# Attention scores of eight units as three one-pass products of high and low parts, held in the rings of the weights

## Chip, cores and metric

One core of a Trainium2 chip runs the whole program in one launch. The metric is the device time in microseconds, the median of the runs. The engines, as the profile names them: PE (matrix products; PEld are its weight loads), DVE (vector), ACT (scalar), POOL (GpSimd), SP (issues the weight transfers). Each engine works through its own list in order and waits on semaphores. PSUM is the memory that PE writes to, in 8 banks of 512 float32 columns.

## The reference

Two model blocks, one behind the other, on 256 latent tokens and (in the first block) 256 context tokens of width 2048, all float32. The first block has two layers with three kinds of attention heads side by side; latent queries read latent and context keys (512), context queries read context keys alone (256). In the second layer the context queries are left out, since nothing reads them.

```python
u = h @ w_in
qa, ka, va, qb, kb, vb, cq, ckv, kpe, z = jnp.split(u, split_points(), axis=-1)
...
# A: 8 heads of 64, neighbourhood window and a bias table; B: 12 heads of 64 over 4 key heads, band, sink
# C: 6 heads of 128 + 64 channels
s_loc = jnp.einsum('bqkgd,bjkd->bkgqj', qi, ki, preferred_element_type=jnp.float32) * scale
s_ctx = jnp.einsum('bqkgd,bckd->bkgqc', qi, kc, preferred_element_type=jnp.float32) * scale
p = jax.nn.softmax(s, axis=-1)
o = p @ v
...
x = x + gate[:, None] * merge_out(o_a, o_b, o_c, z, w_out[l])     # (y * silu(z)) @ w_out
```

The second block (pooling, a short convolution, gates, a feed-forward part of 5632) is not touched by the change.

## The kernel before

*Large products.* Every weight matrix comes in chunks of 128 x 1024 float32 through four buffers (`raw`). A step `split` makes two parts of a chunk: ACT copies it into `whi` in the type float32r (line 1151, the high part), DVE subtracts that from the chunk into `wlo` (line 1566, the low part). Both are rings of three places, `whi[:, s]` and `wlo[:, s]` with s = m % RING for chunk m of the whole program. The activations have high and low parts as well, and a product is the sum of three one-pass products (high x high, high x low, low x high; lines 908 to 910). A place of the ring is free when PE has used the chunk (`used`).

*The plan.* `make_plan` writes one list of steps, and each engine walks through the same list and does its share of each step. So the order in a step list is each engine's order. `pl.split()` puts the next chunk's split there.

*Attention.* A unit is a pair of heads of a kind. There are 13, in the order

```python
UNITS = (("B", 0), ("B", 1), ("C", 0), ("B", 2), ("B", 3), ("C", 1), ("B", 4), ("B", 5), ("A", 0), ("C", 2), ("A", 1),
         ("A", 2), ("A", 3))
```

numbered 0 to 12 here. A unit is worked in slots of 128 queries: in layer 0 four (stream 0, the latent queries, with 512 keys, twice; stream 1, the context queries, with 256 keys, twice), in layer 1 two (512 keys). So layer 0 has 52 slots, layer 1 has 26. For each slot s the plan has the steps `score` and `att`:

- PE, `score(s)`: the two heads' scores, queries x keys, as plain float32 products of 64 rows each (line 1039; kind C at lines 1030 and 1033). It waits for the row maxima of slot s - 2.
- PE, `att(s)`: the values product of slots s - 5 and s - 4 if slot s - 4 ends a stream (lines 1055, 1062), then the transposes of the probabilities of slot s - 2, head 0 and head 1 (line 1081); they wait for the scaled probabilities and for the copies of slot s - 3.
- DVE, `score(s)`: adds the mask and takes the row maximum (line 1982), both heads. `att(s)`: reciprocal of the sums of slot s - 1 (1990), scaling of head 0 (1993), the copy of head 0's transposes of slot s - 2 out of PSUM (2000), and where a unit is finished the product of its output with the gate (2012).
- ACT, `score(s)`: exponentials and sums (1462), both heads. `att(s)`: the copy of head 1's transposes (1471).
- POOL: scales head 1 (2258), sinks and the bias tables of kind A (2208), and issues the transfers of gates (2173).

The queries and keys of kinds A and B lie in `T`, 128 rows by 512 tokens for a pair of heads (two heads of 64 channels).

*The end.* The last three slots also have a `make` step each: the high and low part of an output row for the output projection `wout` (ACT line 1451, DVE line 1969). Then `att` steps alternate with the first chunks of `wout`. The first two splits of `wout` stand behind the two slots of unit 2, stream 0; the third behind the first `att` step after the last slot. During attention nothing else uses the rings.

Of the kernel before, what the change touches and what calls it, by code (L numbers as in the profile page):

```python
# [4 lines left out]
F32 = mybir.dt.float32  # L5
F32R = mybir.dt.float32r
ALU = mybir.AluOpType
ACT = mybir.ActivationFunctionType
# [5 lines left out]
L = 256  # L14
DEPTH = 2
# [23 lines left out]
RING = 3  # L39
# [16 lines left out]
def rows_of(kind, tile):  # L56

    return {"A": [tile], "B": [4 + tile], "C": [10 + 2 * tile, 11 + 2 * tile]}[kind]


Y_ORDER = [y for unit in UNITS for y in rows_of(*unit)]


# [339 lines left out]
def make_plan():  # L403
# [49 lines left out]
    for l, (first, second, third) in enumerate(layers):  # L453
        if l:
            pl.add("scale", l, None)
            pl.seam("layer", l)
            pl.mod_queue(MOD_LAST)
            chunks = pl.chunks(first)
            next(chunks)
            next(chunks)  # L460
            pl.add("load_conditions", 2)
            for _ in chunks:
                g, c = pl.last_chunk
                if g is first[1] and c == 4:
                    pl.add("conditions", 2)
                if g.id > first[1].id and (c % 2 or g.kind in ("kvb", "ka")):
                    pl.mod()
            assert not pl.mods
        pl.add("rq", l)
        pl.latents(second)  # L470
        keys = second[-1]
        pl.left[l], pl.keys[l], pl.queries[l] = pl.owner, keys, second[2]
        pl.turn, pl.owner = 1 - keys.base // 4, {0: None, 4: None}
        slots = slots_of(l)
        pl.add("load_gates", l)
        for s in range(len(slots)):
            pl.add("score", l, slots, s)
            pl.add("att", l, slots, s)
            if s == 0:
                pl.add("key_make", keys, (2, 3))  # L480
            if s == 1:
                pl.add("key_turn", keys, 2)
                pl.add("key_turn", keys, 3)
            if slots[s].unit == 2 and slots[s].stream == 0:
                pl.split()
            if s >= len(slots) - 3:
                pl.add("make", third[0], s - len(slots) + 3)
        chunks = pl.chunks(third, 3)
        for s in range(len(slots), len(slots) + 4):
            pl.add("att", l, slots, s)  # L490
            next(chunks)
        if l == 0:
            pl.mod_queue(MOD_SEAM)
            pl.add("load_conditions", 1)
        pl.add("attended", l, slots)
        for _ in chunks:
            g, c = pl.last_chunk
            if l == 0:
                if g.index == 0 and c == 6:
                    pl.add("conditions", 1)  # L500
                if g.index and (g.index < 3 or c < g.ending):
                    pl.mod(2 if g.index < 3 and c == 0 else 1)
        assert not pl.mods
        pl.flush()
# [11 lines left out]
def build(nc, d):  # L516
# [131 lines left out]

    def key_nope(head):
        return HF[:, head, :]  # L650

    def query_rope(tile):
        return HF[:, 12 + tile, :]
# [153 lines left out]
    def tensor_engine(PE):  # L807
# [210 lines left out]
        def score(l, slots, s):  # L1018
# [8 lines left out]
            if t.kind == "C":  # L1027
# [4 lines left out]
                for h in range(2):  # L1032
                    PE.matmul(out[h], query_rope(t.tile)[half[h], qs], key_rope(t.tile)[half[h], ks], start=False,
                              stop=True, tile_position=(64 * h, 0), skip_group_check=True).then_inc(
                        *scored.up((l, s, h)))
            else:
                q, k = (T_QA + t.tile, T_KA + t.tile) if t.kind == "A" else (T_QB + t.tile, T_KB + t.tile // 3)
                for h in range(2):
                    PE.matmul(out[h], T[half[h], q, qs], T[half[h], k, ks], start=True, stop=True,  # L1039
                              tile_position=(64 * h, 0)).then_inc(*scored.up((l, s, h)))  # L1040
# [101 lines left out]
    def scalar_engine(AC):  # L1142
        def split(m):
            g, c, n = pl.splits[m]
            s = m % RING
            width = min(g.kpc, g.kt - c * g.kpc) * g.width
            AC.wait_ge(*raw_in[pl.homes[n]].at(n))
            if m >= RING:
                was = pl.splits[m - RING]
                AC.wait_ge(*used.at(was[0].id, was[1]))  # L1150
            AC.activation(whi[:, s, 0:width], raw_of(n)[:, 0:width], ACT.Copy).then_inc(*hi.up((g.id, c)))  # L1151

        def ada_row(g):
# [299 lines left out]
        def score(l, slots, s):  # L1453
            t = slots[s]
            st_ = stat[:, s % 4, :, :]
            for h in range(2):
# [4 lines left out]
                    AC.wait_ge(*p_ev.at("sink", l, s))  # L1461
                AC.activation(p_, p_, ACT.Exp, bias=st_[:, 0, h:h + 1], scale=-1.0, accum_out=st_[:, 1, h:h + 1]).then_inc(*exped.up((l, s, h)))

        def att(l, slots, s):
            if 2 <= s < len(slots) + 2:
                t = slots[s - 2]
# [8 lines left out]
        for st in pl.steps:  # L1475
# [43 lines left out]
                att(*st[1:])  # L1519
            elif st[0] == "rq":  # L1520
                latent_roots(st[1])
            elif st[0] == "key_square":
                key_square(*st[1:])
            elif st[0] == "key_root":
# [27 lines left out]
    def vector_engine(VE):  # L1552
# [419 lines left out]
        def score(l, slots, s):  # L1972
            t = slots[s]
            for h in range(2):
# [3 lines left out]
                if t.kind == "A" and t.tile == 0 and t.stream == 0 and h == 0:  # L1978
# [3 lines left out]
                VE.tensor_tensor_reduce(p_of(t, h), PS[:, score_bank(l) + 2 * (s % 2) + h, 0:t.nk], mask_of(t, h), -1.0, first,  # L1982
                                        ALU.add, ALU.min, stat[:, s % 4, 0, h:h + 1]).then_inc(*maxed.up((l, s, h)))

        def att(l, slots, s):
            if 1 <= s <= len(slots):
                t = slots[s - 1]
# [27 lines left out]
        for st in pl.steps:  # L2015
# [43 lines left out]
                att(*st[1:])  # L2059
            elif st[0] == "rq":  # L2060
                VE.tensor_tensor(rq[:, :, 0], rq[:, :, 0], rq[:, :, 1], ALU.add).then_inc(*v_ev.up(("rq_sum", st[1])))
            elif st[0] == "key_square":
                key_square(*st[1:])
            elif st[0] == "key_root":
# [381 lines left out]
```

## Time and profile before

| what | value |
|---|---|
| median of 3 runs | 3156.88 us (3156.69 to 3157.13) |
| profiled execution, its time | 3160.49 us |
| its span | 3159.2 us |
| mean granted PE clock | 0.992 of full speed |
| PE / PEld / DVE / ACT / POOL busy | 98 / 87 / 60 / 42 / 9 % of the span |
| attention, layer 0 | about 692 to 850 us |
| attention, layer 1 | about 1478 to 1578 us |

The page's first part has the busy time of each engine, its second part the span in 40 slices, its fourth the chain of work that ended last, followed back from the end. Timelines list instructions by start in microseconds from the start of the span; "x4" are four records merged, with the time from the first start to the last end; in brackets stands how long the engine was idle before and what released it. A PE record's end is modelled and reaches past the next record's start, so the time that an instruction takes of PE's queue is read from start to start. A float32 product shows as two records. Windows give busy microseconds of each engine in a stretch.

### The profile page before, as it was taken

To read this page: it belongs to the slowest core of one execution; us is meant where nothing else is said; L and a number is where in the kernel's file an instruction comes from. 1 tells how busy PE (TensorE), PEld (TensorE's weight loads), DVE (VectorE), ACT (ScalarE), POOL (GpSimd) and SP (SyncE) were. 2 spreads that over 40 slices of the span, in tenths; PEclk is the share of its full clock that TensorE was granted. 3 is DMA by queue.
4 is the path that set the end of the run, shared out by engine and by line. 5 is a ranking of instruction groups with operands and counts; after the bars stand their busy time and mean duration, and the time that the engine had idled before them with its cause. 6 is when DMAs were issued, how large, how long until landed. Compare 5 with 4: busy or idle time off the path is not lost.

```text
span 3159.2 us, 51244 instructions
## 1 busy us (share of the span) xinstructions
PE 3093.2 (98%) x21274; PEld 2759.7 (87%) x21274; DVE 1893.5 (60%) x2949; ACT 1340.6 (42%) x2075; POOL 295.6 (9%) x386
## 2 busy tenths in 40 slices
PE   7999999999999999998999999999999999999998
PEld 3788888875688898886599999999999999999998
DVE  4376676377768566446757755555556555555445
ACT  4422333355532643345544444344444444444443
POOL 0001000017421010002710000000000000000000
PEclk9999999999999999999999999999999999999999
DMA  9776554221166387432064555555554555555554
GB/s 398 290 236 217 180 192 161 79 74 67 41 253 220 121 300 245 154 112 103 31 204 167 180 184 186 185 190 194 191 193 166 199 194 194 193 195 194 194 194 160
DMA packets 154984, 571.27 MB, mean 181 GB/s; under 512 B 17760, under 2 KB 17888, under 8 KB 152192
## 3 DMA queue, kind: packets, MB, share of 16 engines
q1 hardware_dynamic: 147312, 533.71, 49.2%
q0 software_dynamic: 7440, 34.28, 3.0%
q8 instruction: 168, 2.75, 0.3%
q14 instruction: 64, 0.52, 0.0%
HBM read 555.34 MB, written 12.58 MB: 180 GB/s over the span
## 4 chain that ended last, share of the span: by engine, by line
PE 92%; DVE 2%; DMA 2%; ACT 2%; issue 1%; POOL 1%; SPq 0%; DVEq 0%; ACTq 0%
PE ps L908 20%; PE ps L910 20%; PE ps L909 20%; PE ps L897 7%; PE ps L899 7%; PE ps L898 7%; DMA sb_raw<-in_stream 2%; PE ps L1081 2%; PE ps L1039 1%; PE ps L1062 1%; PE ps L817 1%; PE ps L1055 1%; POOL sb_p L2258 1%; PE ps L1030 1%; DVE sb_p L1982 1%
## 5 line engine op out<-in xcount | busy, mean ns | idle before, releaser
L1566 DVE TENSOR_TENSOR sb_wlo<-sb_raw,sb_whi 128x1024 fp32r<-128x1024 f32 (+1 forms) x809 | 983.5, 1217 | 974.9 <-ACT sb_whi L1151 973.3
L1151 ACT ACTIVATE sb_whi<-sb_raw 128x1024 fp32r<-128x1024 f32 (+1 forms) x813 | 853.9, 1051 | 1030.5 <-PE ps L910 781.0
L908 PE MATMUL ps<-sb_hn_hi,sb_whi 128*128 128x256 f32 (+4 forms) x2944 | 822.3, 279 | 4.4 <-DVE sb_hn_lo L1680 4.4
L909 PE MATMUL ps<-sb_hn_lo,sb_whi 128*128 128x256 f32 (+4 forms) x2944 | 820.9, 279 | 0.0
L910 PE MATMUL ps<-sb_hn_hi,sb_wlo 128*128 128x256 f32 (+4 forms) x2944 | 820.7, 279 | 0.0
L908 PEld LDWEIGHTS ps<-sb_hn_hi,sb_whi 128*128 128x128 f32 x2944 | 555.1, 189 | 5.2 <-DVE sb_hn_lo L1680 4.6
L910 PEld LDWEIGHTS ps<-sb_hn_hi,sb_wlo 128*128 128x128 f32 x2944 | 555.5, 189 | 0.0
L909 PEld LDWEIGHTS ps<-sb_hn_lo,sb_whi 128*128 128x128 f32 x2944 | 555.3, 189 | 0.0
L899 PE MATMUL ps<-sb_whi,sb_lo 128*128 128x512 f32 (+1 forms) x968 | 376.4, 389 | 0.0
L897 PE MATMUL ps<-sb_whi,sb_hi 128*128 128x512 f32 x896 | 356.0, 397 | 5.3 <-DVE sb_lo L1660 4.1
L898 PE MATMUL ps<-sb_wlo,sb_hi 128*128 128x512 f32 x896 | 350.0, 391 | 0.0
L908 PE MATMUL ps<-sb_hi,sb_whi 128*128 128x512 f32 (+1 forms) x992 | 333.1, 336 | 0.3 <-ACT sb_scr L1216 0.2
L909 PE MATMUL ps<-sb_lo,sb_whi 128*128 128x512 f32 (+1 forms) x992 | 330.6, 333 | 0.0
L910 PE MATMUL ps<-sb_hi,sb_wlo 128*128 128x512 f32 (+1 forms) x992 | 330.5, 333 | 0.0
L899 PEld LDWEIGHTS ps<-sb_whi,sb_lo 128*128 128x128 f32 x968 | 183.0, 189 | 37.1
L908 PEld LDWEIGHTS ps<-sb_hi,sb_whi 128*128 128x128 f32 x992 | 186.3, 188 | 26.7 <-issue 5.8
L897 PEld LDWEIGHTS ps<-sb_whi,sb_hi 128*128 128x128 f32 x896 | 169.1, 189 | 39.3 <-DVE sb_lo L1660 4.3
L910 PEld LDWEIGHTS ps<-sb_hi,sb_wlo 128*128 128x128 f32 x992 | 186.3, 188 | 19.5
L909 PEld LDWEIGHTS ps<-sb_lo,sb_whi 128*128 128x128 f32 x992 | 186.4, 188 | 19.0
L898 PEld LDWEIGHTS ps<-sb_wlo,sb_hi 128*128 128x128 f32 x896 | 169.2, 189 | 34.8
L908 PE MATMUL ps<-sb_ffn_hi,sb_whi 128*128 128x256 f32 x688 | 189.9, 276 | 0.0
L910 PE MATMUL ps<-sb_ffn_hi,sb_wlo 128*128 128x256 f32 x688 | 189.9, 276 | 0.0
(306 smaller groups left out, 4270.2 us busy)
## 6 DMA issues: line engine op xcount, KB each, us to landing
sb_raw<-in_stream SPq DMA_DIRECT2D x939, 512.0 KB, 3.4
sb_T<-in_stream SPq DMA_DIRECT2D x41, 512.0 KB, 10.7
sb_raw<-in_stream SPq DMA_DIRECT2D x25, 384.0 KB, 3.0
sb_T<-in_x SPq DMA_DIRECT2D x4, 1024.0 KB, 9.4
z_scratch<-sb_scr POOLq DMA_DIRECT2D x16, 256.0 KB, 3.8
sb_zb<-z_scratch POOLq DMA_DIRECT2D x16, 256.0 KB, 3.0
sb_bias<-in_bias POOLq DMA_DIRECT2D x4, 1024.0 KB, 6.0
x_scratch<-sb_T POOLq DMA_DIRECT2D x4, 1024.0 KB, 4.5
```

What stands on the lines that cost most here:

```text
L817: mm = PE.matmul(PS[t:t + 32, ada_bank(g), :], cond[:, k, :], raw_of(n)[:, 512 * j:512 * j + 512], start=k < 4, stop=k >= 12, tile_positio ...
L897: PE.matmul(o, xh[:, xt], wh, start=k == 0, stop=False)
L898: PE.matmul(o, xh[:, xt], wl, start=False, stop=False)
L899: mm = PE.matmul(o, xl[:, xt], wh, start=False, stop=k == g.kt - 1)
L908: PE.matmul(o, whi[:, s, w], xh, start=k == 0, stop=False)
L909: PE.matmul(o, whi[:, s, w], xl, start=False, stop=False)
L910: mm = PE.matmul(o, wlo[:, s, w], xh, start=False, stop=k == g.kt - 1)
L1030: PE.matmul(out[h], T[:, T_QN + head, qs], key_nope(head)[:, ks], start=True, stop=True, skip_group_check=True)
L1039: PE.matmul(out[h], T[half[h], q, qs], T[half[h], k, ks], start=True, stop=True, tile_position=(64 * h, 0)).then_inc(*scored.up((l, s, h)))
L1081: mm = PE.transpose(PS[:, turn_bank(l, h), kt * P:kt * P + P], p_of(t, h)[:, kt * P:kt * P + P], ident)
L1151: AC.activation(whi[:, s, 0:width], raw_of(n)[:, 0:width], ACT.Copy).then_inc(*hi.up((g.id, c)))
L1566: VE.tensor_tensor(wlo[:, s, 0:width], raw_of(n)[:, 0:width], whi[:, s, 0:width].bitcast(F32), ALU.subtract).then_inc(*lo.up((g.id, c)))
```

## The change

Eight units, all of kind A and those of kind B from tile 2 on (units 3, 4, 6, 7, 8, 10, 11, 12), get high and low parts of their queries and keys. These are put into a place of the rings `whi` and `wlo` (queries in columns 0 to 511, keys in 512 to 1023), and the scores become three one-pass products for each head. ACT makes the high parts in the first slot of the unit before (`operand_hi`), DVE the low parts in the second slot of that unit, stream 0 (`operand_lo`); both steps stand behind `score` and `att` of their slot. PE waits for `operand_lo` before the first score of a changed unit. The two splits of `wout` that stood in unit 2 move to unit 12, the last one, and their ring places wait for the scores of units 10, 11 (and the third one's for those of unit 12). Units 0, 1 and kind C stay as they are.

```diff
+PAIRED = [u for u, (kind, tile) in enumerate(UNITS) if kind == "A" or kind == "B" and tile > 1]
...
-            if slots[s].unit == 2 and slots[s].stream == 0:
+            ahead, first = slots[s].unit + 1, s == 0 or slots[s - 1].unit < slots[s].unit
+            if ahead in PAIRED and first:
+                pl.add("operand_hi", l, ahead)
+            if ahead in PAIRED and not first and slots[s - 1].qt == 0 and slots[s].stream == 0:
+                pl.add("operand_lo", l, ahead)
+            if slots[s].unit == PAIRED[-1] and slots[s].stream == 0:
                 pl.split()
...
+    def operands(l, u):
+        s = (third_first[l].m0 + PAIRED.index(u) + 1 - len(PAIRED) + 2) % RING
+        n, (kind, tile) = L if l else 2 * L, UNITS[u]
+        q, k = (T_QA + tile, T_KA + tile) if kind == "A" else (T_QB + tile, T_KB + tile // 3)
+        return ((T[:, q, 0:n], whi[:, s, 0:n], wlo[:, s, 0:n]),
+                (T[:, k, :], whi[:, s, 512:1024], wlo[:, s, 512:1024]))
+
+    def last_scored(l, u):
+        return scored.at(l, max(t.s for t in slots_of(l) if t.unit == u), 1)
...
+            elif t.unit in PAIRED:                                   # PE, score
+                if t.stream == 0 and t.qt == 0:
+                    PE.wait_ge(*v_ev.at("operand_lo", l, t.unit))
+                (_, qh, ql), (_, kh, kl) = operands(l, t.unit)
+                for i, (q, k) in enumerate(((qh, kh), (qh, kl), (ql, kh))):
+                    for h in range(2):
+                        mm = PE.matmul(out[h], q[half[h], qs], k[half[h], ks], start=i == 0, stop=i == 2,
+                                       tile_position=(64 * h, 0))
+                        if i == 2:
+                            mm.then_inc(*scored.up((l, s, h)))
...
+            if g.kind == "wout" and g.index == 0 and c < RING:       # ACT, split
+                AC.wait_ge(*last_scored(g.layer, PAIRED[c - RING]))
...
+        def operand_hi(l, u):                                        # ACT
+            j = PAIRED.index(u)
+            AC.wait_ge(*(last_scored(l, PAIRED[j - RING]) if j >= RING else used.at("done", pl.keys[l].id)))
+            for v, hi_, _ in operands(l, u):
+                ins = AC.activation(hi_, v, ACT.Copy)
+            ins.then_inc(*a_ev.up(("operand_hi", l, u)))
...
+        def operand_lo(l, u):                                        # DVE
+            VE.wait_ge(*a_ev.at("operand_hi", l, u))
+            for v, hi_, lo_ in operands(l, u):
+                ins = VE.tensor_tensor(lo_, v, hi_.bitcast(F32), ALU.subtract)
+            ins.then_inc(*v_ev.up(("operand_lo", l, u)))
```

## Rows read from the trace of the kernel before

**Rows 1.** The page: busy time, share of the span and instructions of each engine.

```profile
PE 3093.2 (98%) x21274; PEld 2759.7 (87%) x21274; DVE 1893.5 (60%) x2949; ACT 1340.6 (42%) x2075; POOL 295.6 (9%) x386
```

**Rows 2.** The page: chain of work that ended last, by engine.

```profile
PE 92%; DVE 2%; DMA 2%; ACT 2%; issue 1%; POOL 1%; SPq 0%; DVEq 0%; ACTq 0%
```

**Rows 3.** Windows: the attention stretches of both layers.

```profile
core 0: us, PE busy (x) PEld busy (x) DVE busy (x) ACT busy (x) POOL busy (x), PEclk, DMA share, GB/s
691.90:850.20 158.30, 148.51 (x860) 86.03 (x859) 124.23 (x394) 95.22 (x271) 99.05 (x110) 0.98 0.13 44
1478.00:1578.50 100.50, 92.06 (x503) 52.10 (x502) 77.67 (x205) 57.43 (x140) 68.89 (x72) 0.97 0.14 49
```

**Rows 4.** Timeline, layer 1, two units: start, us, engine, line, operation.

```profile
1555.23 1.09 PE L1081 MATMUL ps<-sb_const,sb_p 128*128 128x128 f32 x8
1555.92 0.69 DVE L2000 COPY sb_pt<-ps 128x512 f32<-128x512 f32 x1 [0.56 <-PE ps L1081]
1556.25 1.13 PE L1039 MATMUL ps<-sb_T 64*128 64x512 f32 x4
1556.53 0.42 DVE L2012 TENSOR_TENSOR sb_T<-ps,sb_zb 128x256 f32<-128x256 f32 x1
1557.31 1.09 PE L1081 MATMUL ps<-sb_const,sb_p 128*128 128x128 f32 x8
1559.39 1.95 PE L1062 MATMUL ps<-sb_pt,sb_va 128*64 128x256 f32 x16
1562.29 1.13 PE L1039 MATMUL ps<-sb_T 64*128 64x512 f32 x4
```

**Rows 5.** Timeline, PE, layer 0: scores of 256 keys, then transposes.

```profile
776.39 0.70 PE L1039 MATMUL ps<-sb_T 64*128 64x256 f32 x4
777.03 1.09 PE L1081 MATMUL ps<-sb_const,sb_p 128*128 128x128 f32 x8
```

**Rows 6.** Windows: one-pass products, of 512 and of 256 columns.

```profile
875.00:900.00 25.00, 25.00 (x112) 20.72 (x111) 8.37 (x9) 12.27 (x12) 4.35 (x5) 1.00 0.85 349
3000.00:3100.00 100.00, 100.00 (x885) 100.00 (x884) 49.77 (x51) 42.69 (x46) 5.17 (x7) 1.00 0.56 193
```

**Rows 7.** Timeline: weight loads of one slot's scores.

```profile
1556.25 0.30 PEld L1039 LDWEIGHTS ps<-sb_T 64*128 64x128 f32 x4 [0.17 <-issue]
```

**Rows 8.** Lines 1969 and 1451: ns min/median/max; then one of 256.

```profile
L1969 DVE TENSOR_TENSOR sb_lo<-sb_T,sb_hi x16: 680/684/693, 844.0 to 884.4; 128x512 fp32r<-128x512 f32 x16
L1451 ACT ACTIVATE sb_hi<-sb_T x16: 613/617/624, 843.3 to 883.0; 128x512 fp32r<-128x512 f32 x16
1571.00 0.42 DVE L1969 TENSOR_TENSOR sb_lo<-sb_T,sb_hi 128x256 fp32r<-128x256 f32 x1
```

**Rows 9.** Windows: one unit of kind A in layer 0.

```profile
827.91:837.74 9.83, 9.72 (x66) 5.29 (x65) 8.75 (x31) 6.84 (x20) 6.91 (x6) 1.00 0.18 56
```

**Rows 10.** Timeline, layer 1, unit 2: a split behind slot 5.

```profile
1500.76 1.04 ACT L1151 ACTIVATE sb_whi<-sb_raw 128x1024 fp32r<-128x1024 f32 x1
1500.94 1.23 PE L1081 MATMUL ps<-sb_const,sb_p 128*128 128x128 f32 x8
1501.84 1.22 DVE L1566 TENSOR_TENSOR sb_wlo<-sb_raw,sb_whi 128x1024 fp32r<-128x1024 f32 x1 [0.87 <-ACT sb_whi L1151]
1502.98 0.74 DVE L1982 CUSTOM_DVE_ANT_0 sb_p<-ps,sb_const,sb_nsink 128x512 f32<-128x512 f32 x1
```

**Rows 11.** Timeline: transposes ahead of the first output-projection chunk, both layers.

```profile
849.77 0.41 PE L1081 MATMUL ps<-sb_const,sb_p 128*128 128x128 f32 x2 [1.67 <-DVE sb_pt L2000]
1577.40 1.39 PE L1081 MATMUL ps<-sb_const,sb_p 128*128 128x128 f32 x8 [1.32 <-DVE sb_T L2000]
```

**Rows 12.** Timeline and windows: two gaps of PE and the clock.

```profile
697.47 0.41 PE L959 MATMUL ps<-sb_const,sb_lo_f 128*128 128x128 f32 x2 [3.60 <-DVE sb_lo_f L1869]
700.20:703.60 3.40, 3.15 (x14) 1.77 (x13) 2.85 (x10) 2.01 (x7) 2.60 (x3) 0.50 0.00 0
748.00:751.50 3.50, 1.82 (x12) 0.97 (x11) 3.26 (x6) 2.23 (x8) 3.50 (x6) 1.00 0.06 23
```

More of the change, by code:

```diff
@@ L650, in key_nope @@
         return HF[:, head, :]
+    def operands(l, u):
[6 more added lines that the diff above has]
+        return scored.at(l, max(t.s for t in slots_of(l) if t.unit == u), 1)
+    third_first = [next(g for g in pl.groups if g.kind == "wout" and g.layer == l) for l in range(DEPTH)]
     def query_rope(tile):
@@ L1035, in score @@
                         *scored.up((l, s, h)))
+            elif t.unit in PAIRED:
[8 more added lines that the diff above has]
+                            mm.then_inc(*scored.up((l, s, h)))
             else:
-                q, k = (T_QA + t.tile, T_KA + t.tile) if t.kind == "A" else (T_QB + t.tile, T_KB + t.tile // 3)
+                q, k = T_QB + t.tile, T_KB + t.tile // 3
                 for h in range(2):
@@ L1521, in scalar_engine @@
                 latent_roots(st[1])
+            elif st[0] == "operand_hi":
+                operand_hi(*st[1:])
             elif st[0] == "key_square":
@@ L2061, in vector_engine @@
                 VE.tensor_tensor(rq[:, :, 0], rq[:, :, 0], rq[:, :, 1], ALU.add).then_inc(*v_ev.up(("rq_sum", st[1])))
+            elif st[0] == "operand_lo":
+                operand_lo(*st[1:])
             elif st[0] == "key_square":
```

## The prediction, made before the changed kernel was built

> **What bounds the kernel now.** First the page's busy line and its chain of waits: the matrix engine (PE) works 98% of the span and is 92% of the chain [rows 1, 2]. A change pays only if it shortens PE's queue or keeps it from waiting. Then the two attention stretches: 158.3 us in layer 0 and 100.5 us in layer 1, PE busy 148.5 and 92.1 of them, the vector engine (DVE) 124.2 and 77.7 [rows 3]. So PE leads, but DVE is a close second at 78%. Last the timeline around one step from unit to unit in layer 1, because the change puts DVE work there [rows 4]: transposes of slot 17 at 1555.23, first score of the next unit at 1556.25, its transposes 1557.31, values 1559.39, the next unit's first score 1562.29. In these 6.04 us stand two scores of 1.06, two sets of transposes of 1.02 and, as the rest, values of 1.88. No PE row there carries a wait of weight; the 6.04 us of a unit are PE's own work.
>
> **Part 1, the scores.** One slot's scores are two float32 products of 64 rows, which the trace shows as four PE records that share the array in pairs. With 512 keys they take 1.06 us of PE's queue (1556.25 to 1557.31 [rows 4]), with 256 keys 0.64 us (776.39 to 777.03 [rows 5]). The difference is 0.42 us for 256 columns, which leaves about 0.21 us fixed. New are six one-pass products, three for each head. A one-pass product takes 25.0/112 = 0.223 us at 512 columns and 100/885 = 0.113 us at 256 [rows 6], so the float32 product streams its keys about four times, the new one three times. If the heads go on sharing the array, a slot takes 3/4 x 0.85 + 0.21 = 0.85 us and 3/4 x 0.43 + 0.21 = 0.53 us, so 0.21 and 0.11 us less. Changed are 8 units: 2 slots of 512 keys in each layer (32), 2 of 256 in layer 0 (16). Gross gain 32 x 0.21 + 16 x 0.11 = 8.5 us, 3.4 of it in layer 1. If the six ran in series it would be 6 x 0.223 + 0.21 = 1.55 and 6 x 0.113 + 0.21 = 0.89 us, a loss of 0.49 and 0.25 each, 19.7 in all: the other bound. I take the overlap, because the float32 records of the same tile positions show it.
>
> The weight loads are the doubtful point. The four loads of a slot's scores lie within 0.30 us of its start [rows 7], two for each half of the array, so a half takes a second load while its first product still streams. The Trainium skill, "TensorE: Matmul & The Clock Gate", section "Measured speedup vs the span model", says that a load overlaps running matmuls only when its row group differs. By that rule the second and third loads of a half would be exposed, and the gain would vanish; the 0.30 us speak against it here.
>
> **Part 2, the high and low parts.** For each unit the scalar engine (ACT) copies queries and keys, DVE subtracts. One piece of 512 columns costs DVE 0.68 us, of 256 0.42 us, ACT 0.62 us for 512 [rows 8]; started behind each other they take some 0.07 us less. Layer 0 (512 + 512): DVE 1.3 us. Layer 1 (256 + 512): 1.03 us. ACT's copies go into the first slot of the unit before and need about 1.0 to 1.2 us; after its last copy ACT waits for a score and a row maximum (0.85 + 0.1 + 0.6 us), so I cost them at 0 to 0.1.
>
> The place of the subtraction decides. It stands at the end of DVE's list for the second slot of the unit before, behind the copy of the transposes (L2000) and the gate product (L2012), and PE waits for it ahead of the next unit's first score.
>
> *Layer 1* has one stream, so that score is the very next thing PE does after those transposes. From their start at 1555.23: the copy can start at 1555.92, when the first half is through, the gate product at 1556.53 [rows 4], the subtractions at 1556.9, done at 1557.95, PE released at about 1558.05 instead of 1556.25. A stall of 1.8 us. Behind the stopped PE stand both scores, both sets of transposes and the values of the unit, and DVE has nothing to do until that score is there, so neither catches up. New period: 0.85 + 1.02 + 0.85 + 1.88 + 2.82 (to the release) = 7.42 us for 6.04, +1.4. Eight such steps: 8 x 1.8 = 14.6, and 0.66 more where the gated unit is of kind C (a second gate product [rows 4], 0.33 us behind the first, at two of the steps): 15.3 us. Less 16 x 0.21 = 3.4: **+11.9**.
>
> *Layer 0* has two streams, so two slots of 256 keys lie between subtraction and use; PE need not wait for it directly. But DVE is busy 8.75 us of a 9.83 us unit [rows 9]. With 1.3 more it has 10.05: DVE becomes the bound in the five units of kind A or B that carry a subtraction (3, 6, 7, 10, 11): +0.2 each at least, +0.3 taken for idle time that it can't fill, 1.5. Their score gain is gone in that figure. Units 4, 8 and 12 carry none and keep 2 x 0.21 + 2 x 0.11 = 0.64 each: -1.9. Units of kind C have long PE work and hide it. Layer 0: **-0.4** (all hidden would be -5.1; +0.5 a unit more, +0.6).
>
> **Part 3, the moved splits.** Two splits of output-projection chunks move from unit 2 to unit 12. Each is 1.05 us on ACT, then 1.22 us on DVE, which waits for ACT. In layer 1 at unit 2 the next row maximum starts at 1502.98, 2 us after its score ended at 1500.94 [rows 10]. Taking these away gives back 0.7 and 0.8 us. At unit 12 they hit the drain of the pipeline, where PE already waits 1.67 and 1.32 us for DVE's copies [rows 11]. Following the queue in layer 1: the subtraction puts the row maximum of slot 25 2.05 us later, so the copy of slot 23, so the transposes of slot 24; chunk 0 follows. **+2**. In layer 0 both splits stand before the row maxima of slots 49 and 50, each costs some 2 us and little is idle: **+4**. Their two loads are issued later too, but while DMA is little used (mean share 0.13 and 0.14 [rows 3]): 0. The bounds for both are nothing and 2 x 2.3 us a layer.
>
> **Sum** on the profiled span of 3159.2 us: layer 0 -0.4 + 4 - 0.7 = +2.9; layer 1 +11.9 + 2 - 0.8 = +13.1; together +16, a span of 3175. The profiled execution itself took 3160.49 us, 3.6 over the median of the runs, 3156.88; I put the difference on the median: **3173 us**, 0.5% slower.
>
> **Rivals.**
> *The clock falls (15%).* The moved splits stretch PE's waits at the ends of attention to about 3.0 and 3.4 us. A wait of 3.60 us at 697.47 was followed by a granted clock of 0.50 [rows 12], 1.2 GHz. A fall costs about half of 6.8 us: 3.4 us, two of them 6.8: 3176 to 3180. The 1.8 us stalls leave PE busy three quarters of the time; a stretch with 1.82 busy of 3.50 us kept clock 1.00 [rows 12], so I expect none there. The Trainium skill, "TensorE: Matmul & The Clock Gate", section "Why this matters for your kernels", advises against idle gaps over some 3 us between bursts of matmuls; the 3.60 us row agrees.
> *The six products don't overlap (7%).* Then the scores lose 19.7 us instead of gaining 8.5. Layer 1 pays it in full (16 x 0.70 = 11), layer 0 partly behind DVE (about 10): +37, near 3194. For it: no row has one-pass products on half the array. Against it: the pairs and the loads [rows 5, 7].
> *Half the stall (8%).* If DVE's queue is ahead of where I put it and the stall is near 0.9 us, layer 1 costs 5 us and the moved splits little: within 0.2%, 3158 to 3163.
> *Faster (4%).* The other side: the subtraction falls in time in which DVE is idle. Then only the 8.5 us count, 3148. It decides from the point where the subtractions end before the second half of the transposes, 0.5 us after the first. The copy ahead of them alone needs more [rows 4], so this wants another order of DVE's work than the code has.
> *The sum (66%)*, 3165 to 3182: half to one and a half times the split costs, the layer 1 stall at 1.6 to 2.2 us, and layer 0 from -3 to +3 beside it.
>
> The range 3164 to 3187 takes in the clock's case and leaves out 8% + 4% below and 7% above. 0.2% is 6.3 us, about what a measurement tells from no change: slower by more has 0.66 + 0.15 + 0.07 = 0.88, same 0.08, faster 0.04.
>
> **What the profile after would show.** Right: PE's first score of each changed unit in layer 1 waits some 1.8 us for DVE's subtraction, eight times, and the layer 1 stretch grows by 13 us to about 114; a changed slot of 512 keys takes about 0.85 us; in layer 0 those scores wait for nothing, units 6, 7, 10, 11 take about 10.1 us, with DVE nearly full; the waits before chunk 0 grow to 3 us or more. Wrong: slots of 1.2 us or more (no overlap), a granted clock of 0.50 inside layer 1's units, or waits under 1 us at the new scores. What could break it most: a DVE queue that runs in another order than I read.

## The result: 0.9% slower, in the place that was forecast, by more than was forecast

The changed kernel took 3184.27 us (median of 4 runs, 3179.5 to 3209.13), the kernel before beside it 3157.01 (3156.69 to 3158.66): ratio 1.0095, 95% interval 1.0056 to 1.0134. The forecast was 3173 us, a ratio of 1.005. Slower is right; 3184 lies inside the range of 3164 to 3187 and 11 us above its centre, and the ratio that the forecast stands for lies outside the interval.

The profiled execution of the changed kernel took 3179.5 us (span 3178.2). The page's busy line and its chain of waits, which answer to [rows 1] and [rows 2]:

```profile
PE 3092.3 (97%) x21370; PEld 2770.1 (87%) x21370; DVE 1909.5 (60%) x2981; ACT 1356.2 (43%) x2107; POOL 296.6 (9%) x386
...
PE 93%; DVE 3%; ACT 1%; issue 1%; DMA 1%; POOL 1%; SPq 0%; DVEq 0%; ACTq 0%
```

PE is busy as long as before in a span 19 us longer, so on the whole the added time is waiting. (Its busy time has slower products in it as well, as the filler experiment shows below.) The windows of the two attention stretches, from the first score to the first output-projection chunk, say where; under them four short windows of layer 1:

```profile
core 0: us, PE busy (x) PEld busy (x) DVE busy (x) ACT busy (x) POOL busy (x), PEclk, DMA share, GB/s
691.90:855.30 163.40, 148.12 (x923) 92.03 (x923) 133.37 (x411) 103.27 (x287) 99.67 (x110) 0.96 0.13 43
1478.30:1597.90 119.60, 96.16 (x544) 60.02 (x543) 82.95 (x221) 64.71 (x157) 69.59 (x72) 0.92 0.11 37
1510.00:1512.40 2.40, 1.42 (x8) 0.90 (x9) 1.13 (x3) 1.11 (x3) 2.40 (x4) 0.83 0.00 0
1512.40:1515.80 3.40, 3.40 (x16) 2.50 (x15) 2.68 (x8) 2.01 (x5) 2.55 (x4) 0.62 0.15 41
1530.50:1532.90 2.40, 0.79 (x4) 0.76 (x6) 1.46 (x2) 0.00 (x0) 1.65 (x4) 0.83 0.06 14
1532.90:1536.30 3.40, 3.40 (x19) 2.19 (x16) 2.50 (x7) 1.74 (x5) 0.93 (x1) 0.62 0.08 29
```

Layer 0's attention grew from 158.3 us [rows 3] to 163.4. Layer 1's took 102.2 us before (cut in the same way, from the first score at 1476.4; the window of [rows 3] begins 1.6 us after that score) and 119.6 after. Together that is +22.5 us where the forecast had +16. PE's granted clock over layer 1's stretch is 0.92 for 0.97, and the short windows show two of its falls, each at the end of a wait of PE.

The waits of PE in layer 1, by line; columns: engine and line, what was waited for, us in total, times, longest:

```profile
PE ps L1061 <- DVE sb_wlo L2028: 15.9, 8, 2.7
PE ps L978 <- DVE sb_lo_f L1909: 3.6, 1, 3.6
PE ps L1110 <- DVE sb_T L2046: 3.0, 1, 3.0
PE ps L1110 <- DVE sb_pt L2046: 0.7, 1, 0.7
```

L1061 is the new score, L2028 the subtraction `operand_lo`: eight waits, 15.9 us, as forecast (eight, 15.3). The wait of 3.0 us is the one for the last transposes, 1.32 before [rows 11]. The timeline shows first an undisturbed step, to be read against [rows 4], and then a disturbed one:

```profile
1567.83 1.09 PE L1110 MATMUL ps<-sb_const,sb_p 128*128 128x128 f32 x8
1568.52 0.69 DVE L2046 COPY sb_pt<-ps 128x512 f32<-128x512 f32 x1 [0.56 <-PE ps L1110]
1569.13 0.41 DVE L2058 TENSOR_TENSOR sb_T<-ps,sb_zb 128x256 f32<-128x256 f32 x1
1569.46 1.02 DVE L2028 TENSOR_TENSOR sb_wlo<-sb_T,sb_whi 128x256 fp32r<-128x256 f32 x2
1570.63 0.50 PE L1061 MATMUL ps<-sb_whi 64*128 64x512 f32 x2 [1.70 <-DVE sb_wlo L2028]
1571.52 1.09 PE L1110 MATMUL ps<-sb_const,sb_p 128*128 128x128 f32 x8
1578.11 0.51 PE L1061 MATMUL ps<-sb_whi 64*128 64x512 f32 x2 [1.70 <-DVE sb_wlo L2028]
...
1528.30 1.09 PE L1110 MATMUL ps<-sb_const,sb_p 128*128 128x128 f32 x8
1529.60 0.42 DVE L2058 TENSOR_TENSOR sb_T<-ps,sb_zb 128x256 f32<-128x256 f32 x1
1529.83 1.58 POOL L2256 TENSOR_TENSOR sb_bias<-sb_bias,sb_const 128x256 f32<-128x256 f32 x2
1529.93 2.03 DVE L2028 TENSOR_TENSOR sb_wlo<-sb_T,sb_whi 128x256 fp32r<-128x256 f32 x2
1532.11 0.80 PE L1061 MATMUL ps<-sb_whi 64*128 64x512 f32 x2 [2.72 <-DVE sb_wlo L2028]
1533.69 1.95 PE L1110 MATMUL ps<-sb_const,sb_p 128*128 128x128 f32 x8
```

In the first, DVE does its copy, its gate product and the subtraction behind each other after the transposes of 1567.83, and PE has nothing to do until 1570.63: a wait of 1.70 us and a unit of 7.48 us (1570.63 to 1578.11) for 6.04. Scores to transposes take 0.89 us (1570.63 to 1571.52) where the old ones took 1.06, so the products of the two heads do share the array (six in series would take 6 x 0.223 = 1.34 [rows 6]). In the second, the subtraction takes 2.03 us instead of 1.02 with POOL's L2256 running beside it. The wait is 2.72 us, and what follows runs at half the clock: 1.58 us for the slot's scores, 1.95 for eight transposes that take 1.09 above.

### The profile page after: what moved, and what is told of

Its sections match the earlier page's. It is cut to its first block, busy times and chain, and to the rows that moved or that the text cites. A ratio compares the mean times of both kernels' runs of the same rounds, so it can differ in the third digit from the quotient of the medians.

```text
span 3178.2 us, 51516 instructions
## 1 busy us (share of the span) xinstructions
PE 3092.3 (97%) x21370; PEld 2770.1 (87%) x21370; DVE 1909.5 (60%) x2981; ACT 1356.2 (43%) x2107; POOL 296.6 (9%) x386
## 4 chain that ended last, share of the span: by engine, by line
PE 93%; DVE 3%; ACT 1%; issue 1%; DMA 1%; POOL 1%; SPq 0%; DVEq 0%; ACTq 0%
PE ps L927 20%; PE ps L929 20%; PE ps L928 20%; PE ps L916 7%; PE ps L918 7%; PE ps L917 7%; PE ps L1110 2%; PE ps L1091 1%; PE ps L836 1%; PE ps L1061 1%; DMA sb_raw<-in_stream 1%; PE ps L1049 1%; PE ps L1084 1%; PE ps L1009 1%; DVE sb_wlo L1606 1%
```

## The experiments

The time of a whole run is a blunt measure here: runs of one kernel, the one before among them, differ by 30 us and more from one to the next, through a part that the change doesn't touch (last section). The lengths of the two attention stretches repeat within about a microsecond where the clock does. So each kernel is judged by them first. The table gives the time in us from the first score to the first output-projection chunk in one profile each, and in brackets how much of it passed at a granted clock of 0.50. The kernel before has a second profile to see how far the stretches repeat: they differ from the first by 0.8 and 0.9 us.

| kernel | layer 0 | layer 1 | sum | ratio of times (95%) |
|---|---|---|---|---|
| before | 158.3 (6.8) | 102.2 (6.8) | 260.5 | 1 |
| before, again | 159.1 (10.2) | 101.3 (0) | 260.4 | |
| changed | 163.4 (13.7) | 119.6 (18.0) | 283.0 | 1.0095 (1.0056 to 1.0134) |
| changed, second | 162.8 (17.6) | 116.4 (6.8) | 279.2 | 1.0096 (1.0052 to 1.0139) |
| changed, fourth | 164.1 (13.2) | 120.0 (17.6) | 284.1 | |
| changed, fifth | 163.4 (17.0) | 120.6 (23.9) | 284.0 | |
| subtraction early | 163.3 (10.8) | 100.4 (6.0) | 263.7 | 0.9988 (0.9955 to 1.0022) |
| splits moved alone | 161.3 (9.5) | 101.4 (3.6) | 262.7 | 1.0036 (0.9999 to 1.0072) |
| filler products | 164.2 (13.2) | 113.6 (5.4) | 277.8 | 1.0039 (1.0004 to 1.0074) |
| filler products, again | 163.4 (13.7) | 113.6 (5.1) | 277.0 | |
| plain scores, waits kept | 165.5 (11.3) | 117.8 (4.6) | 283.3 | 1.0109 (1.0048 to 1.0171) |
| layer 0 alone | 163.6 (9.8) | 103.0 (6.8) | 266.6 | 1.0015 (0.9991 to 1.0039) |
| layer 1 alone | 159.2 (10.2) | 119.9 (17.4) | 279.1 | 1.0063 (1.0030 to 1.0095) |
| layer 1 alone, again | 158.1 (6.8) | 119.5 (18.0) | 277.6 | |
| layer 1 alone, filler | 158.1 (6.8) | 113.2 (0) | 271.3 | 1.0028 (0.9987 to 1.0068) |
| six units, early | 159.0 (10.2) | 99.6 (3.4) | 258.6 | 1.0007 (0.9978 to 1.0035) |
| six units, layer 1 alone | 158.7 (6.8) | 99.5 (3.4) | 258.2 | 0.9998 (0.9958 to 1.0037) |

### The changed kernel again, and the subtraction moved forward

Two experiments on the main claim. The first is the changed kernel itself.

> The changed kernel as it is, once more, timed in more rounds. If the excess over the forecast 3173 us is a fixed cost, the runs lie close together near 3184 us. If part of it is the granted clock falling in the 1.7 us gaps, or a transfer that comes late in some runs, the runs spread by 5 to 30 us as the first four did (3179.5 to 3209.1 us), and their mean clocks differ.

The ratio came out the same, 1.0096, and the times spread as in the second case of the expectation, from 3182.75 to 3224.21 us (two more of the twelve ran at another clock throughout, see the last section). The profile has the same eight waits (16.6 us) but only one fall of the clock between units, and a layer 1 of 116.4 us.

The second does the same work at another place: copies two units ahead, subtraction at the start of the unit before.

```diff
             if ahead in PAIRED and first:
-                pl.add("operand_hi", l, ahead)
-            if ahead in PAIRED and not first and slots[s - 1].qt == 0 and slots[s].stream == 0:
                 pl.add("operand_lo", l, ahead)
+            if ahead + 1 in PAIRED and not first and slots[s - 1].qt == 0 and slots[s].stream == 0:
+                pl.add("operand_hi", l, ahead + 1)
```

> Only the place of the two steps is changed: the subtraction moves from the second slot of the unit before to its first slot, the copies one slot further ahead (second slot of the unit before that). The work is the same. Theory (the place makes the stall): PE's waits for the subtraction (15.9 us, 8 times in layer 1) go, and the falls of the clock inside layer 1 with them; scores keep their gain; about 3160 us, 3157 to 3164. Rival (the amount of work on the vector engine): no better than 3175 us. Rival (something outside attention became slower): layer 1's stretch gets shorter, the time stays above 3170 us.

Layer 1 fell to 100.4 us, below the kernel before, and the ratio to 0.9988; the median of 3167.20 us is above the 3157 to 3164 expected, but so is that of the kernel before beside it (3164.86). DVE does as much there as in the changed kernel (83.69 us of the stretch for 82.95), so it is the place of the subtraction, not its amount, that costs layer 1 its time. No score waits for DVE any more; the waits of PE in layer 1 and one unit of the timeline:

```profile
PE ps L1110 <- DVE sb_T L2046: 4.3, 3, 3.4
PE ps L978 <- DVE sb_lo_f L1909: 3.6, 1, 3.6
PE ps L1110 <- DVE sb_pt L2046: 1.3, 2, 0.7
...
1555.38 1.09 PE L1110 MATMUL ps<-sb_const,sb_p 128*128 128x128 f32 x8
1556.41 0.49 PE L1061 MATMUL ps<-sb_whi 64*128 64x512 f32 x2
1557.30 1.09 PE L1110 MATMUL ps<-sb_const,sb_p 128*128 128x128 f32 x8
1562.12 0.50 PE L1061 MATMUL ps<-sb_whi 64*128 64x512 f32 x2
```

The unit takes 5.71 us (1556.41 to 1562.12) for 6.04 before. Layer 0 stayed at 163.3, but not because the place does nothing there. Units 2 to 10 took 111.7 us (714.56 to 826.29) for 113.3 in the changed kernel and 111.9 with the moved splits alone. Unit 11 then took 12.29 us for 9.98, with a wait of 1.20 us for DVE's copy at 832.95 and a fall of the clock at 834.2.

### The moved splits alone

The kernel before, with the two splits at unit 12:

```diff
-            if slots[s].unit == 2 and slots[s].stream == 0:
+            if slots[s].unit == 12 and slots[s].stream == 0:
```

> The kernel before with the two splits of the output projection moved from unit 2 to unit 12 alone, no high and low parts of queries and keys. Theory: +6 us in the drains (4 in layer 0, 2 in layer 1), -1.5 us at unit 2, so about 3161 us. Rival: the moved splits cost nothing, 3157 us.

Layer 0 took 161.3 us (+3.0 on the first profile, +2.2 on the second), layer 1 101.4, no change. The median was 3175.53 us beside 3164.86, where +4.5 had been expected; its interval reaches from nothing to 0.7%. Behind the first score of unit 12, layer 0 took 16.96 us (836.21 to 853.17) for 12.46, which is +4.5 for the +4 expected in that drain. PE's wait for the last transposes of layer 1 grew from 1.32 us [rows 11] to 3.1, as the forecast had it. What was given back behind unit 2 paid for it: units 3 and 4 of layer 1 took 14.62 us for 16.44 in the second profile of the kernel before, 1.8 us less where 0.8 had been expected.

### Filler in the gaps: what the clock costs

PE runs two products that nobody reads in each of layer 1's eight waits. Their results are not used; everything else is as in the changed kernel.

```diff
                 if t.stream == 0 and t.qt == 0:
+                    if l:
+                        for _ in range(2):
+                            PE.matmul(PS[:, pl.keys[l].base + 3, :], ident, const[:, band0:band0 + 512], start=True, stop=True)
                     PE.wait_ge(*v_ev.at("operand_lo", l, t.unit))
```

> The changed kernel with PE kept busy in layer 1 while it waits for the subtraction: two float32 products of 512 columns (0.85 us each) on constants into an unused PSUM bank, ahead of each of the eight waits. They do no useful work. Theory (the excess over the forecast is the clock, which falls in the gaps): no granted clock of 0.50 between the units of layer 1, about 1.7 us less for each of the four falls of the changed kernel's profile, so 7 us less than the changed kernel and less spread between runs. Rival: the excess has another cause, then the time stays or grows by what the two products reach past the wait (0 to 3 us).

The trace shows these as plain float32 products, 1.88 us for the two, so they fill nearly the whole wait. The filler kernel's waits, a step of its timeline and its window of layer 1:

```profile
PE ps L1064 <- DVE sb_wlo L2031: 2.4, 5, 0.9
...
1548.79 1.04 PE L1113 MATMUL ps<-sb_const,sb_p 128*128 128x128 f32 x8
1549.67 1.88 PE L1059 MATMUL ps<-sb_const 128*128 128x512 f32 x4
1551.77 0.50 PE L1064 MATMUL ps<-sb_whi 64*128 64x512 f32 x2 [0.22 <-DVE sb_wlo L2031]
...
1482.30:1595.90 113.60, 103.74 (x575) 60.95 (x575) 83.33 (x221) 64.38 (x157) 69.12 (x72) 0.98 0.11 39
```

The first score comes 2.98 us after the start of the transposes (1548.79 to 1551.77); the same step without filler takes 3.07 (1549.05 to 1552.12). The wait is as long as ever, only filled. But no fall stands between two units any more, and layer 1 is 6.0 us shorter than in the first profile of the changed kernel, for the 7 expected. The two left are behind the wait for L1912 at the start, which the first profile of the kernel before has as well, and in the drain. Timed in the same set the ratios are 1.0039 and 1.0096, the same direction, with intervals that overlap.

Whether those falls are the usual case took more profiles.

> The change in layer 1 alone, and PE runs two one-pass products of 512 columns on a free bank while it would wait for the subtraction, ahead of each new unit's first score; nothing else differs from only_l1. Theory, the clock: in only_l1 layer 1's attention took 119.9 us with 17.1 us of it at a granted clock of about 0.5; with the gaps filled no fall stands between two units, at most that of the drain, and the stretch takes 113 to 115 us, as in the kernel with both layers and the filler (113.6); the timed median is 5 to 9 us under that of only_l1. Rival, the falls cost nothing of note, since the waits for DVE leave room for a slower PE: the stretch stays over 117 us, the time within 2 us of only_l1.

> The changed kernel with the filler products in layer 1's gaps, a second profile. Theory: no fall between units in any execution, 113 to 114.5 us for layer 1's attention, as in both profiles with a filler so far (113.6, 113.2). Rival, the filler's executions had luck: 116 us or more.

> The change in layer 1 alone, a second profile. Theory, falls are usual: 117 to 120 us for layer 1's attention with 10 us or more at the low clock. Rival: 114 to 116.5 us. Layer 0 158 to 159.5 us, as before the change.

> The changed kernel, a third profile. It says how often the clock falls between the units of layer 1 (17.2 us at the low clock in the first profile, 6.8 in the second). Theory, the falls are the usual case and cost about 3 us on top of the waits: layer 1's attention 116 to 120 us, with three or more falls between units. Rival, they were one execution's: 114 to 116.5 us and at most one fall. Layer 0 162 to 164 us in both.

> The changed kernel once more. Theory, the falls of the clock between the units of layer 1 are the usual case: layer 1's attention 117 to 120 us, 10 us or more of it at the low clock. Rival, they are rare: 114 to 116.5 us, at most 7 us at the low clock. Layer 0 162 to 164 us in both.

> The changed kernel once more, with the same two cases: 117 to 120 us for layer 1's attention with 10 us or more at the low clock, or 114 to 116.5 us with at most 7.

The third profile of the changed kernel can't be compared in length: that whole execution ran at a mean granted clock of 0.748 and took 3882.65 us. There too the clock fell further, to 0.50, behind five of the eight waits. The others settle it. Without filler five of six profiles have four or more falls of 3.4 us between units, and take 119.5 to 120.6 us; the sixth has one fall of 6.8 and takes 116.4. With filler, three of three have none and take 113.6, 113.6 and 113.2. The expectation of layer 1 alone with filler calls the filler products one-pass; they were not, as said. Timed, that kernel has a ratio of 1.0028 where layer 1 alone has 1.0063, again in the expected direction and with intervals that overlap. The windows of layer 1, changed kernel (fourth and fifth profile), layer 1 alone again, then layer 1 alone with filler:

```profile
1481.10:1601.10 120.00, 96.16 (x543) 59.59 (x543) 83.07 (x222) 64.59 (x157) 69.81 (x72) 0.93 0.11 37
```
```profile
1481.20:1601.80 120.60, 98.71 (x543) 61.53 (x543) 82.76 (x221) 64.55 (x157) 69.36 (x72) 0.90 0.11 37
```
```profile
1477.40:1596.90 119.50, 96.06 (x542) 59.91 (x542) 82.84 (x222) 64.59 (x157) 69.46 (x72) 0.92 0.11 37
```
```profile
1475.70:1588.90 113.20, 101.90 (x576) 59.57 (x575) 82.99 (x221) 64.25 (x157) 69.11 (x72) 1.00 0.11 39
```

In the last, PE's 101.90 us hold eight fillers of 1.88, so the kernel's own work is 86.9 us at clock 1.00. The same work takes 96.1 at 0.92: 9.2 us of slower products. The stretch is 6.3 us shorter (119.5 to 113.2), so about two thirds of the slower work reaches the end and the rest is taken out of waits.

### Plain scores, waits kept

The copies, the subtractions and all waits stay; the scores are the old float32 products.

```diff
-                for i, (q, k) in enumerate(((qh, kh), (qh, kl), (ql, kh))):
-                    for h in range(2):
-                        mm = PE.matmul(out[h], q[half[h], qs], k[half[h], ks], start=i == 0, stop=i == 2,
-                                       tile_position=(64 * h, 0))
...
+                (q, _, _), (k, _, _) = operands(l, t.unit)
+                for h in range(2):
+                    PE.matmul(out[h], q[half[h], qs], k[half[h], ks], start=True, stop=True,
+                              tile_position=(64 * h, 0)).then_inc(*scored.up((l, s, h)))
```

> The changed kernel with the scores left as plain float32 products; the copies, subtractions, waits and moved splits stay. Theory (a slot of 512 keys takes 0.89 us of PE instead of 1.06, and in layer 1 all of it counts): layer 1's attention 16 x 0.17 = 2.7 us longer than in the changed kernel, layer 0's 0 to 2 us. Rival (the new products bring nothing): both stretches as in the changed kernel, 163 and 116 to 120 us.

PE's waits for the subtraction are the same:

```profile
PE ps L1060 <- DVE sb_wlo L2025: 16.2, 8, 2.7
```

Layer 1 takes 117.8 us, with one fall between units. The expected 2.7 us more than in the changed kernel did not come as a difference of stretches, since the falls differ: 117.8 lies under the first profile's 119.6 and above the second's 116.4. Units 10 and 11, which no fall touches in either trace, show it without them: 7.82 and 9.77 us for 7.48 and 9.43 in the changed kernel, 0.34 a unit or 0.17 a slot, the difference of 1.06 and 0.89. Sixteen slots make 2.7. In layer 0 the new scores are worth 2.1 (165.5 to 163.4). The gain forecast for them exists. The fewer falls say nothing about the scores: the second profile of the changed kernel has one as well. In both of these the clock stays up behind the first wait of layer 1 (3.6 us, L978); in the five with four falls or more it falls there. Why, the runs don't show.

### One layer at a time

The change with `l in (0,)` or `l in (1,)` at its five places, the other layer as before.

> The change in layer 0 alone; layer 1 as before, its splits in unit 2. Theory: layer 0's attention about 163 us (before 158.3), of it 3 from the moved splits; layer 1's 102. In all +5 us. Rival (layer 0 costs nothing, the 5 us come with the state of the clock): layer 0 near 158 us.

> The change in layer 1 alone; layer 0 as before. Theory: layer 1's attention 114 to 120 us (before 102.2), by how often the clock falls in it; layer 0's 158. In all +13 to +18 us, so layer 1 carries three quarters of the whole effect. Rival: under +8 us.

The two layers' costs stand by themselves: 163.6 us for layer 0 with layer 1 near its old length (103.0), 119.9 for layer 1 with layer 0 at its old (159.2). Four fifths of the loss is layer 1's.

### A version that should win

Early placement, six units in place of eight and the splits at unit 9, away from the drain; then the same in layer 1 alone.

```diff
-PAIRED = [u for u, (kind, tile) in enumerate(UNITS) if kind == "A" or kind == "B" and tile > 1]
+PAIRED = [u for u, (kind, tile) in enumerate(UNITS) if kind == "A" and tile < 2 or kind == "B" and tile > 1]
...
-            if slots[s].unit == PAIRED[-1] and slots[s].stream == 0:
+            if slots[s].unit == 9 and slots[s].stream == 0:
```

> A version meant to be better: six units instead of eight (3, 4, 6, 7, 8, 10), the subtraction in the first slot of the unit before as in the kernel 'early', and the two splits in unit 9, whose long PE work covers them. Theory: layer 1's attention 16 - 4 = 12 slots x 0.17 = 2 us less than before, so about 100; layer 0's near 159, since DVE is nearly full there; together 0 to 2 us faster than before. Rival (the subtractions crowd DVE wherever they stand): layer 0 at 161 or more, no gain in all.

> Layer 1 alone, six units in place of eight, the subtraction at the start of the unit before (its copies a unit earlier), and the splits at unit 9; layer 0 as before. Theory, place and not amount: the new products keep their gain of 0.15 to 0.2 us a slot, no score waits for DVE, layer 1's attention takes 99.5 to 100.5 us for 102.2, layer 0's 158 to 159, and the time is 2 us under the kernel before (3155). Rival, DVE's added work costs as much as the scores gain wherever it stands: layer 1 at 102 to 103 us, the time equal to the kernel before.

In the profiles both are about 2 us shorter than before over attention (258.6 and 258.2 for 260.4), nearly all of it in layer 1, 99.6 and 99.5 us for 101.3 to 102.2. Timed, that is less than 0.1% and can't be told from nothing: ratios 1.0007 and 0.9998. No version was measured as faster than the kernel before.

## Why the prediction was right in direction and too small

The sum by its own terms, with the mean of four profiles after (163.4 and 119.2 us) against the mean of two before (158.7 and 101.8): forecast +2.9 and +13.1, measured +4.7 and +17.4.

**The stall in layer 1: right.** Eight waits, 15.9 us for 15.3; the undisturbed one 1.70 for 1.8. The chain copy, gate product, subtraction is the one forecast, and moving the subtraction removed it. The two steps with a second gate product wait 2.03 and 2.04, as forecast. Not forecast were two longer ones, 2.32 and 2.72 us; the second is a subtraction that doubled beside POOL work. (Eight times 1.8 is 14.4, not the 14.6 of the prediction; the slip adds 0.2 us to its sum.)

**The scores: right in kind, a little less in size.** 0.89 us a slot for a forecast 0.85, so 0.17 instead of 0.21 gained. The rival of products in series is out: it would have made 1.55. In the trace the third pair of products starts 0.23 us behind the second (1570.93, 1571.16), as close as products stand in [rows 6], and its weights are loaded meanwhile. The Trainium skill's rule in "TensorE: Matmul & The Clock Gate" (it stands in the section "The mechanism"), by which loads of the same row group don't overlap and which the prediction took to cancel this gain, is not borne out by that and by slots of 0.89 us.

**Layer 1 without the clock: slightly over.** The filler's three profiles give 113.5 us, +11.7 for a forecast +13.1. Of the difference 1.0 is the splits' time given back behind unit 2, 1.8 us for 0.8.

**The clock in layer 1: the step that failed.** It is the sentence "The 1.8 us stalls leave PE busy three quarters of the time; [...] so I expect none there." It argued from one stretch of [rows 12] that kept clock 1.00 with 1.82 of 3.50 us busy, and took that for a rule. The second profile of the kernel before has the same work at the same place, with a wait of 1.61 us in it, and there the clock falls right behind:

```profile
747.50:751.00 3.50, 1.84 (x13) 0.98 (x12) 3.25 (x6) 2.24 (x8) 3.50 (x6) 1.00 0.07 29
751.40:754.80 3.40, 3.40 (x16) 1.59 (x14) 2.63 (x10) 1.57 (x5) 3.40 (x6) 0.50 0.03 7
```

So one profile of the kernel before was not enough to rule a fall out. Six profiles with the new waits show the clock falling between units of layer 1, up to six times, behind waits of 1.7 to 2.7 us; filling the waits removed the falls and 5.9 us (mean of six without, 119.3, against 113.5). A clock of 0.50 inside layer 1's units is also what the prediction named as a sign of being wrong. The clock's rival stood at 15% and only at the drains. Of the 6.1 us that attention took beyond the forecast, layer 1 has 4.3: 5.7 for the clock (119.2 against 113.5), less the 1.4 by which the rest was forecast too high. The other 1.8 are layer 0's. The Trainium skill's "TensorE: Matmul & The Clock Gate", section "Why this matters for your kernels", which puts the danger at gaps over some 3 us, would have missed these as well: every one of the eight gaps is shorter.

**Layer 0: the sign of the small term was wrong.** Units 3, 6, 10 and 11 grew by 0.1 to 0.2 us (12.11, 12.11, 12.01 and 9.98 us for 11.88, 11.88, 11.88 and 9.83) and unit 7 by 0.5 (10.59 for 10.06). In size that is about what was forecast, in part by luck: 3, 6 and 10 never were units of 9.8 us that become 10.1, and in unit 6 DVE is busy 10.75 of the 12.11 us, so it is not the bound there. But units 4, 8 and 12 did not keep their score gains: unit 4 with unit 5 took 27.42 us (742.49 to 769.91) for 26.87. Up to unit 12's first score layer 0 had lost 1.1 us, where the same terms of the forecast have it 0.5 ahead. In units 4 and 7 the wait of PE that grew ends with ACT, not DVE:

```profile
745.24 0.41 PE L1110 MATMUL ps<-sb_const,sb_p 128*128 128x128 f32 x2 [1.39 <-ACT sb_pt L1509]
786.49 1.14 ACT L1499 ACTIVATE sb_whi<-sb_T 128x512 fp32r<-128x512 f32 x2
789.46 0.63 PE L1110 MATMUL ps<-sb_const,sb_p 128*128 128x128 f32 x4 [1.16 <-ACT sb_ptc L1509]
```

Before, these waits were 0.60 us and none. In unit 7 the high parts (L1499, 1.14 us) stand ahead of ACT's exponential and copy, which the prediction costed at 0 to 0.1 us. In unit 4 ACT's exponential waits for POOL (2.49 us at 743.52). No run takes these two apart from DVE's work, and how much of layer 0's excess is theirs stays open. DVE is as full as forecast in the unit of kind A; here from unit 11 to the end of the drain:

```profile
828.88:839.10 10.22, 9.72 (x75) 6.10 (x76) 10.03 (x34) 7.93 (x24) 7.25 (x7) 1.00 0.15 54
839.10:855.30 16.20, 12.09 (x76) 7.63 (x75) 12.65 (x35) 10.46 (x26) 6.68 (x6) 0.79 0.27 82
...
846.88 2.12 PE L1110 MATMUL ps<-sb_const,sb_p 128*128 128x128 f32 x8 [2.57 <-DVE sb_ptc L2046]
854.92 0.63 PE L1110 MATMUL ps<-sb_const,sb_p 128*128 128x128 f32 x4 [1.53 <-DVE sb_pt L2046]
```

**The moved splits: near in sum.** From unit 12's first score to chunk 0 layer 0 took 16.44 us (838.86 to 855.30) for 12.46: +4.0, where the splits' +4 less unit 12's own 0.6 makes +3.4; the splits alone made +4.5. The waits in layer 0 are 2.57 and 1.53 us, not 3 or more (layer 1's is 3.0), and behind the first stands a fall of the clock (the window's 0.79). Every version with the splits at unit 12 of layer 0 has one within the last 10 us of that attention, none with them elsewhere: the clock's rival as it was put. Its price is not separate, since the stretch is no shorter where the fall comes only 3 us before its end (163.6 in the version with layer 0 alone, 164.1 in the fourth profile). In layer 1 the splits alone cost nothing that can be measured, for a forecast +1.2 net, since more was given back than forecast.

**What is left over.** Attention accounts for 22 us of the 27 between the medians. The other 5 lie in code that is the same in both kernels, and whose length changes between executions by more than that. I didn't pursue them further.

## What to carry to other kernels

When two engines hand work to and fro with nothing else to run, an operation appended to the end of the other engine's list is paid for in full at every step, even if that engine has idle time to spare; put it where the waiting engine is busy, a step earlier, and it can be free, as in layer 1 here. A repeated wait of PE costs more than its length if the clock falls behind it: look at the granted clock between the waits in a trace that has such waits, and don't infer from one gap that the next will keep it. A gain of 0.2 us a slot needs a place with a free engine: in layer 0, where DVE was 89% busy in a unit of kind A, neither place for the subtraction kept it.

## What the runs showed of the hardware

**Short waits can bring the clock down.** Behind waits of 1.70 to 2.72 us the granted clock fell to 0.50 for 3.4 us, at the same four steps in five profiles (about 34, 54, 64 and 75 us into layer 1's attention), and with the waits filled it fell at none of them in three. Two more profiles with the same waits, one of them with plain scores, had one fall each. The step at 34 us can fall without a long wait: the version with layer 0 alone, whose layer 1 is the old one, has a fall at 1515.1 behind waits of 0.65, 0.66 and 0.92 us.

**DVE slows beside POOL.** The two subtractions of a step take 1.02 us alone and 2.03 beside POOL's L2256; a scaling (L2039) of 0.49 us took 1.07 beside it (1507.90). Not all POOL work does it: next to POOL's scaling L2306 the two subtractions took 1.01 us (1509.82). The Trainium skill, "Advanced Engine Details and Errata", section "GPSIMD Details", names a cause that fits the subtraction, which reads two SBUF tiles: the two engines share a read and a write interface, and DVE instructions with two SBUF inputs conflict on it. By that alone L2306 should have disturbed it too, so this trace agrees in part only, and no run here separates the cause from others.

**One-pass products of 256 columns have two rates.** In the long dense stretch of products behind attention, with PE 100% busy at clock 1.00, 100 us hold 884 or 885 of them [rows 6], or 852. The same window, of the kernel before and then of the one with the early subtraction:

```profile
2100.00:2200.00 100.00, 100.00 (x884) 100.00 (x884) 51.80 (x56) 45.59 (x55) 0.00 (x0) 1.00 0.57 193
```
```profile
2100.00:2200.00 100.00, 100.00 (x852) 100.00 (x851) 51.21 (x57) 46.44 (x57) 0.00 (x0) 1.00 0.57 187
```

How many such stretches an execution has varies: from layer 1's first output-projection chunk to the end the profiles take 1576.4 to 1608.3 us, with the same code. That is most of the spread between executions, and it hides effects of a few microseconds. What chooses the rate stays open.

**A whole execution can run at a lower clock.** The third profile of the changed kernel has a granted clock of 0.75 throughout, 707 products in 100 us instead of 885, and 3882.65 us. Of the twelve timed executions that gave the ratio 1.0096, one took 3882.80 us at a mean granted clock of 0.75 and one 5178.74 us at 0.56; both are left out of it. Why they ran so stays open.
